# State-space norm: squares of the prompt columns summed between the two halves of the heads' products, sample columns handled apart

## What is computed

```python
# Mamba-2
y = y + xs * D_skip
y = y.reshape(B, T, SSM_DIM) * silu(z)
yg = y.reshape(B, T, SSM_GROUPS, SSM_DIM // SSM_GROUPS)            # 2 groups of 512 channels
yg = yg * rsqrt(mean(yg * yg, axis=-1, keepdims=True) + NORM_EPS)
out = yg.reshape(B, T, SSM_DIM) * norm_w
# RWKV-7, per head of 64 channels
yn = (y - mean(y)) * rsqrt(var(y) + RW_LN_EPS) * ln_w + ln_b
out = (yn + bonus) * g
```

## Time and profile before

| | |
|---|---|
| median of 3 runs | 4482.1 us (4466.71 to 4493.42) |
| profiled execution | 4487.48 us, its span 4485.9 us |
| busy over the span | PE 94%, PEld 85%, DVE 72%, ACT 32%, POOL 35% |
| mean granted clock of TensorE over the span | 0.969 |
| changed function | 1253.2 to 1394.0 us |
| busy in 1253.2 to 1394.3 | PE 96.7, PEld 59.0, DVE 69.4, ACT 67.8, POOL 37.5 us |
| granted clock of TensorE in it | 0.69 |

### The profile page before, as it was taken

One profiled execution on the slowest core, in us unless ns is written; L12 is line 12 of the kernel. 1 busy time (PEld: TensorE's weight loads), 2 busy tenths in 40 slices (PEclk: granted clock), 3 DMA queues, 4 the chain that ended last, 5 costly groups with the idle time before them and its releaser, 6 DMA issues. The chain is left out here.

```text
span 4485.9 us, 85731 instructions
## 1 busy us (share of the span) xinstructions
PE 4205.8 (94%) x32575; PEld 3817.0 (85%) x32575; DVE 3225.6 (72%) x6008; ACT 1431.1 (32%) x2183; POOL 1565.5 (35%) x1316
## 2 busy tenths in 40 slices
PE   7989998999768979999999998899999999999997
PEld 4888887888546868978878887899999999999996
DVE  5631344555844237899985664999999999999997
ACT  2211222111634222233346765222222222222223
POOL 6333333564031200044443323444343443433431
PEclk9999999999868989999999999999999999999998
DMA  4655665455543311134434455999999999999994
GB/s 169 201 193 187 203 226 205 172 200 182 138 140 97 130 73 39 39 127 143 143 125 174 174 210 190 331 302 299 301 300 302 301 302 295 304 303 296 305 299 158
DMA packets 523006, 928.01 MB, mean 207 GB/s; under 512 B 284032, under 2 KB 351232, under 8 KB 518688
## 3 DMA queue, kind: packets, MB, share of 16 engines
q1 hardware_dynamic: 387024, 549.29, 37.3%
q0 software_dynamic: 80960, 346.96, 22.6%
q10 hardware_dynamic: 54816, 28.85, 2.2%
HBM read 785.79 MB, written 206.30 MB: 221 GB/s over the span
## 5 line engine op out<-in xcount | busy, mean ns | idle before, releaser
L3271 POOL DMA_INDIRECT ex_rows<-expert_rows,ex_here x512 | 588.0, 1148 | 952.2 <-DVE acc_tok L3406 861.0
L3406 DVE SCALAR_TENSOR_TENSOR acc_tok<-ex_rows,ex_wsp,acc_tok 128x1024 f32<-128x1024 f32 x512 | 633.5, 1278 | 0.0
L2650 PE MATMUL ex_psa<-x_dense_high,eg_u_high 128*128 128x288 f32 x2048 | 604.5, 295 | 13.9 <-DVEq L3460 13.9
L2741 POOL TENSOR_TENSOR eg_u_low<-eg_u,eg_u_high 128x1024 fp32r<-128x1024 f32 x130 | 330.0, 2539 | 808.4 <-ACT eg_u_high L2736 808.4
L2650 PE MATMUL ex_psa<-x_dense_low,eg_u_high 128*128 128x288 f32 x2048 | 604.5, 295 | 0.0
L2650 PE MATMUL ex_psa<-x_dense_high,eg_u_low 128*128 128x288 f32 x2048 | 604.2, 295 | 0.0
L3303 PE MATMUL ex_pso<-ex_w_high,ex_v_high 128*128 128x288 f32 x2048 | 441.4, 297 | 11.7 <-DVE acc L3388 6.6
L3334 ACT ACTIVATE ex_w<-ex_psa 128x288 f32<-128x288 f32 x256 | 105.5, 412 | 1062.8 <-PE ex_psa L2650 1060.3
L3303 PE MATMUL ex_pso<-ex_w_high,ex_v_low 128*128 128x288 f32 x2048 | 440.0, 297 | 0.0
L3303 PE MATMUL ex_pso<-ex_w_low,ex_v_high 128*128 128x288 f32 x2048 | 438.9, 296 | 0.0
L3388 DVE TENSOR_TENSOR acc<-ex_pso,acc 128x576 f32<-128x576 f32 x512 | 373.7, 750 | 47.9 <-PE ex_pso L3303 47.9
(11 more groups left out here) (514 smaller groups left out, 9533.7 us busy)
## 6 DMA issues: line engine op xcount, KB each, us to landing
eg_u<-in_u SPq DMA_DIRECT2D x256, 512.0 KB, 3.3
expert_rows<-in_v SPq DMA_DIRECT2D x128, 512.0 KB, 7.0
ex_v<-in_v SPq DMA_DIRECT2D x128, 512.0 KB
weights<-wt_stage SPq DMA_DIRECT2D x9, 4096.0 KB, 12.2
ex_g<-weights SPq DMA_DIRECT2D x128, 288.0 KB
expert_rows<-eg_act SPq DMA_DIRECT2D x256, 128.0 KB, 1.7
proj<-in_out POOLq DMA_DIRECT2D x50, 548.5 KB, 6.2
in_w<-in_w_in SPq DMA_DIRECT2D x50, 512.0 KB, 4.7
```

Source lines behind the costliest of these rows:

```text
L2650: yield nc.tensor.matmul(out[:, 0:b - a], w[:, kc, :], half[:, kc, a:b], start=n == 0, stop=n == len(passes) - 1)
L2741: self.k.nc.gpsimd.tensor_tensor(self.ul[par][:, :, :], self.u[par % 2][:, :, :], self.uh[par][:, :, :].bitcast(F32), ALU.subtract).then_i ...
L3271: pool.indirect_dma_start(rows[i][:, :], None, table, index(here[par][:, t, j:j + 1]), element_offset=ROW_RUNS[t][0]).then_inc(s_row[i], 16)
L3406: v.scalar_tensor_tensor(out=acc_tok[:, t, :], in0=rows[i][:, at:at + D], scalar=wsp[:, i:i + 1], in1=acc_tok[:, t, :], op0=ALU.mult, op1= ...
```

## The change

The prompt columns and the sample columns of the Mamba-2 norm are parted. The squares of the prompt columns go in place over silu(z), which is no longer needed once a tile is gated (so no buffer is waited for), and their sums into two PSUM banks of 512 columns. The samples' squares are made in one instruction, summed in eight products of 64 columns into the bank that held the heads' result, and scaled in eight small instructions of their own. The arena is only as large as the sample recurrence needs. The orders are rewritten: on SP the load of S comes first; on TensorE the heads run in two halves of eight with only `mean(0)` between them, then `var(0)` and the first four sums with `mean(1)`, then the states; on ScalarE the centred square of pair 0 and two squares stand behind sigmoids 0 to 3, sigmoids 4 to 7 come before `rw_rstd(0)`; on VectorE "skip" comes before `gated(0)`.

```diff
@@ -1807,10 +1807,12 @@
         col = sb("col", [P, 3, SH])
         cb = sb("cb", [P, SG, L])
         btok = sb("btok", [P, SG, SN])
-        arena = sb("arena", [P, 3 * T])
+        arena = sb("arena", [P, SH * (SD + 2 * L)])
         heads_of = lambda at, n: arena[:, at:at + SH * n].rearrange("p (h m) -> p h m", h=SH)
         xt, w, ce = heads_of(0, SD), heads_of(SH * SD, L), heads_of(SH * (SD + L), L)
-        sq, rs = [arena[:, i * T:(i + 1) * T] for i in range(2)], arena[:, 2 * T:3 * T]
+        sq = [z[:, i, 0:SEQ] for i in range(KC)]
+        rs = [z[:, GT * g, 0:SEQ] for g in range(SG)]
+        sq_s, rs_s = z[:, :, SEQ:T], z[:, 0:SG, SEQ:T]
         xd = sb("xd", [P, SH, SD])
         end = sb("end", [P, NSEQ, SH])
         xm = [sb(f"xm{i}", [P, SH, SD]) for i in range(2)]
@@ -1818,11 +1820,12 @@
         rw_rs = sb("rw_rs", [P, T])
         ps = ctx.enter_context(nc.psum_tensor("ss_ps", [P, 2, 512], F32))
         ps_so3 = ctx.enter_context(nc.psum_tensor("po_so_ps", [P, 3, 512], F32))
-        ps_so, ps_rw = banked(ps_so3), banked(ctx.enter_context(nc.psum_tensor("po_rw_ps", [P, 3, 512], F32)))
+        ps_so, ps_rw = flat(ps_so3[:, 1:3, :]), banked(ctx.enter_context(nc.psum_tensor("po_rw_ps", [P, 3, 512], F32)))
         cview = ps[:, 0, 0:3 * SH].rearrange("p (q h) -> p q h", q=3)
         bcv = ps[:, 1, :].rearrange("p (i g m) -> p i g m", i=2, g=SG)
         xv = ps_so3[:, 0:2, :].rearrange("p a b -> p (a b)").rearrange("p (h m) -> p h m", h=SH)
         yv = ps_so3[:, 0, :].rearrange("p (a l) -> p a l", a=KC)
+        sum_s = ps_so3[:, 0, 0:SG * L]
         s_S = k.sem("ss_state_loaded")
         s_out = k.sem("ss_state_stored")
         s_xm = k.sem("ss_masked_x")
@@ -1832,7 +1835,9 @@
         s_skip = k.sem("ss_y_gated")
         s_gp = k.sem("so_prompt_gated")
         s_r = k.sem("so_rstd_step")
-        s_n = k.sem("so_scaled")
+        s_sq = k.sem("so_samples_squared")
+        s_sum = k.sem("so_samples_summed")
+        s_rs = k.sem("so_samples_rstd_step")
         PE = Progress(k.sem("ss_pe"), "col", "bc", "x", "y")
         AC = Progress(k.sem("ss_act"), "excs", "col", "btok", "dec")
         DV = Progress(k.sem("ss_dve"), "cb", "x", "diff", "end", "ce", "xd", "w", "skip")
@@ -1848,8 +1853,8 @@
         with nc.Block() as block:
             @block.sync
             def _(sp):
+                sp.dma_start(S[:, :, :, :].rearrange("p s h m -> p s (h m)"), io["ssmT"].rearrange("s n m -> n s m")).then_inc(s_S, 16)
                 rw_post_load(k, sp, 0, y, gate, bonus)
-                sp.dma_start(S[:, :, :, :].rearrange("p s h m -> p s (h m)"), io["ssmT"].rearrange("s n m -> n s m")).then_inc(s_S, 16)
                 rw_post_load(k, sp, 1, y, gate, bonus)
                 mw.load(sp, 0, mw.wa, mw.wb, mw.s_w)
                 for p_ in range(2, NPAIR):
@@ -1896,7 +1901,16 @@
                     pe.wait_ge(SQ.sem, SQ.done("sq", i))
                     if i == GT:
                         pe.wait_ge(s_r, 1)
-                    product(ps_so, k.ones[:, :], sq[i % 2], i % GT == 0, i % GT == GT - 1).then_inc(*SP.inc("sum"))
+                    for a, b in ((0, 512), (512, SEQ)):
+                        mm = nc.tensor.matmul(ps_so[:, a:b], k.ones[:, :], sq[i][:, a:b], start=i % GT == 0, stop=i % GT == GT - 1)
+                    mm.then_inc(*SP.inc("sum"))
+
+                def total_samples():
+                    pe.wait_ge(s_sq, 1)
+                    for i in range(KC):
+                        mm = nc.tensor.matmul(sum_s[:, L * (i // GT):L * (i // GT) + L], k.ones[:, :], sq_s[:, i, :],
+                                              start=i % GT == 0, stop=i % GT == GT - 1)
+                    mm.then_inc(s_sum, 1)
 
                 def heads(lo, hi):
                     for i in range(lo, hi):
@@ -1928,38 +1942,37 @@
                 for i in range(KC):
                     mm = nc.tensor.transpose(xv[0:L, 2 * i:2 * i + 2, :].rearrange("p h m -> p (h m)"), inx[:, i, :], k.ident[:, :])
                 mm.then_inc(*PE.inc("x"))
-                mean(0)
                 pe.wait_ge(s_S, 16)
                 at(DV, "w")
-                heads(0, 4)
+                heads(0, 8)
+                mean(0)
+                heads(8, 16).then_inc(*PE.inc("y"))
                 var(0)
-                heads(4, 8)
+                total(0)
+                total(1)
                 mean(1)
-                heads(8, 12)
-                var(1)
-                heads(12, 16).then_inc(*PE.inc("y"))
-                mean(2)
+                total(2)
+                total(3)
                 at(AC, "btok")
                 at(DV, "xd")
                 states(0)
-                total(0)
                 states(1)
-                total(1)
+                var(1)
+                total(4)
+                total(5)
+                total_samples()
+                mean(2)
+                states(2)
+                states(3)
+                total(6)
+                total(7)
                 var(2)
-                states(2)
-                total(2)
-                states(3)
+                states(4)
+                states(5)
                 mean(3)
-                total(3)
-                states(4)
-                total(4)
-                states(5)
+                states(6)
+                states(7)
                 var(3)
-                total(5)
-                states(6)
-                total(6)
-                states(7)
-                total(7)
 
             @block.scalar
             def _(act):
@@ -1991,17 +2004,24 @@
 
                 def square(i):
                     act.wait_ge(s_gp, i + 1)
-                    if i >= 2:
-                        act.wait_ge(SP.sem, SP.done("sum", i - 2))
-                    a.activation(sq[i % 2], ob[:, i, :], ACT.Square).then_inc(*SQ.inc("sq"))
+                    a.activation(sq[i], ob[:, i, 0:SEQ], ACT.Square).then_inc(*SQ.inc("sq"))
+
+                def square_samples():
+                    act.wait_ge(s_skip, 1)
+                    a.activation(sq_s, ob[:, :, SEQ:T], ACT.Square).then_inc(s_sq, 1)
 
                 def so_rstd(g):
                     act.wait_ge(SP.sem, SP.done("sum", GT * g + GT - 1))
-                    if g:
-                        act.wait_ge(s_n, GT)
-                    a.activation(rs, ps_so[:, 0:T], ACT.Ln, scale=1.0 / (GT * P), bias=k.const[:, 0:1]).then_inc(s_r, 1)
+                    a.activation(rs[g], ps_so[:, 0:SEQ], ACT.Ln, scale=1.0 / (GT * P), bias=k.const[:, 0:1]).then_inc(s_r, 1)
                     act.wait_ge(s_r, 2 * g + 1)
-                    a.activation(rs, rs, ACT.Exp, scale=-0.5).then_inc(s_r, 1)
+                    a.activation(rs[g], rs[g], ACT.Exp, scale=-0.5).then_inc(s_r, 1)
+
+                def so_rstd_samples():
+                    act.wait_ge(s_sum, 1)
+                    a.activation(rs_s, sum_s.rearrange("p (g l) -> p g l", g=SG), ACT.Ln, scale=1.0 / (GT * P),
+                                 bias=k.const[:, 0:1]).then_inc(s_rs, 1)
+                    act.wait_ge(s_rs, 1)
+                    a.activation(rs_s, rs_s, ACT.Exp, scale=-0.5).then_inc(s_rs, 1)
 
                 act.wait_ge(smp.s_in, 48)
                 a.activation(ce, csb[:, :, :], ACT.Exp).then_inc(*AC.inc("excs"))
@@ -2014,40 +2034,41 @@
                 sigmoid(1)
                 at(DV, "diff")
                 a.activation(w[0:L, :, :], w[0:L, :, :], ACT.Exp).then_inc(*AC.inc("dec"))
-                centered_square(0)
                 sigmoid(2)
                 sigmoid(3)
-                rw_rstd(0)
-                centered_square(1)
+                centered_square(0)
+                square(0)
+                square(1)
                 sigmoid(4)
                 sigmoid(5)
-                rw_rstd(1)
+                square(2)
+                square(3)
+                sigmoid(6)
+                sigmoid(7)
+                rw_rstd(0)
+                square_samples()
                 at(DV, "xd")
                 masked_x(0)
                 masked_x(1)
-                sigmoid(6)
-                sigmoid(7)
-                centered_square(2)
-                act.wait_ge(s_skip, 1)
-                square(0)
-                square(1)
-                masked_x(2)
-                rw_rstd(2)
-                masked_x(3)
-                square(2)
-                square(3)
-                masked_x(4)
-                centered_square(3)
-                masked_x(5)
+                centered_square(1)
                 so_rstd(0)
                 square(4)
                 square(5)
-                rw_rstd(3)
-                masked_x(6)
-                masked_x(7)
+                rw_rstd(1)
+                masked_x(2)
+                masked_x(3)
+                centered_square(2)
                 square(6)
                 square(7)
                 so_rstd(1)
+                so_rstd_samples()
+                rw_rstd(2)
+                masked_x(4)
+                masked_x(5)
```

(45 more changed lines are left out.)

## The result

| | before | after |
|---|---|---|
| median of 16 runs | 4492.36 us (4466.71 to 4499.72) | 4505.24 us (4487.78 to 4512.72) |
| ratio after / before | | 1.0029, 95% interval 1.0019 to 1.0039 |
| profiled execution, its span | 4487.48, 4485.9 us | 4506.03, 4504.4 us |
| changed function | 1253.23 to 1394.27: 141.0 us | 1252.30 to 1413.89: 161.6 us |
| granted clock in it | 0.69 | 0.62 |

The kernel became 12.9 us slower, 0.29%. Most of the difference between the forecast of 4494 and the measured 4505.24 is the base: the three runs that the forecast started from had a median of 4482.1, the sixteen have 4492.36. The difference itself was forecast at +11.4 and measured at +12.9. In the two profiled executions the function differs by more, 20.6 us, 9 us above the forecast. Where those 9 us come from is the subject of much of what follows; why the medians show less of them stays open in part.

What follows compares the result with a forecast made beforehand. No engine bounds the function; a chain of releases hopping between engine queues does. Its six legs from 1269.6 end the block at 1405.4, 11.4 us later than before, giving 4494 us (+0.27%), range 4468 to 4512.

Steps and rivals of the forecast that it cites:

- Start: SP's load of S, now issued first, lands near 1266; heads then wait for VectorE's `w` and start 2.1 us earlier.
- Leg 1: Heads to `center(0)`: eight uninterrupted heads at the low clock, 2.21 us each, then `mean(0)` and `center(0)`; 22.9 us.
- Rival 2: Clock rises in unbroken heads: six of the first eight take 1.28 us, `mean(0)` 2.0; total 4486; chance 0.06.
- Leg 2: ScalarE from the centred square through squares, table loads and four sigmoids to `rw_rstd(0)`; 21.6 us.
- Leg 3: VectorE from `gated(0)` to `center(1)`: 7.6 us of work plus 8.0 of exclusion by POOL's decays of S; 15.6 us.
- Leg 4: ScalarE from `center(1)` to `gated(1)`: squares, `so_rstd(0)` and `rw_rstd(1)`, with TensorE and VectorE work hidden; 12.7 us.
- Legs 5 and 6: `gated(1)` through `rw_rstd(2)`, 27.3 us; then `gated(2)` to the block's end, 35.7 us, TensorE's clock partly low.
- rival 3: TensorE's broken tail stays at the low clock, `states(3)` held up by 6 us; +25, total 4507; chance 0.17.
- Rival 4: New order does what it is arranged for, waits overlap; block ends 7.6 us earlier, total 4475; chance 0.10.

Runs made afterwards that it cites:

- one-element decays: Changed kernel with POOL's eight decays of S cut to one element each (sample states then wrong); 4491.61 us, ratio 1.0001 to the kernel before.
- additions first: Changed kernel with add_state(4) ahead of gated(2) and scale(1), and the samples' rstd and scaling later; 4493.26 us, ratio 1.0013 to before.
- tail filled: Changed kernel with 13 unread products of 512 columns put into TensorE's idle time in the tail; 4495.99 us, ratio 1.0015 to before.
- decays later: Changed kernel with POOL's decays held until gate_prompt(5) is done; 4503.16 us, ratio 1.0050 to the kernel before.
- rearranged kernels: Two kernels keeping the changed kernel's split, with norm products between heads and additions ahead of scalings; 4463.15 and 4455.89 us, ratios 0.9941 and 0.9939 to before.
- rearranged further: First of the rearranged kernels with gated(1) ahead of the skip and total(2) ahead of the last four heads; 4455.89 us, ratio 0.9939 to before.

## Why the prediction held, step by step

The legs of the prediction beside the same stretches in the profile of after, each from the end of one named instruction to that of the next; all from the start of the heads, forecast at 1269.6 and found at 1268.8 in a function that began 0.9 us earlier.

| leg | forecast | measured |
|---|---|---|
| 1: eight heads, `mean(0)`, `center(0)` | 22.9 | 22.9 |
| 2: ScalarE, to the rstd of pair 0 | 21.6 | 23.9 |
| 3: VectorE beside the decays | 15.6 | 15.7 |
| 4: to the rstd of pair 1 | 12.7 | 12.7 |
| 5: to the rstd of pair 2 | 27.3 | 29.0 |
| 6: to the end | 35.7 | 40.6 |
| sum | 135.8 | 144.8 |

**Start.** As said: the load of S goes out first, at 1252.3, and lands in time, after 12.8 us, and VectorE's `w` is what releases the heads.

**Leg 1.** As said, to 0.1 us: 2.2 us a head, and `mean(0)` at the low level. Rival 2, a clock that rises inside unbroken heads, falls: the windows have 0.50 over 39.2 us in which TensorE never idles. The rule cited from the Trainium skill, "TensorE: Matmul & The Clock Gate", Part 1, disagrees with the trace here: the heads do not lift the clock.

**Leg 2.** Two errors of opposite sign. No table was loaded between the squares and `sigmoid(4)`: 1.3 us less. But the last eight heads were all slow, where the sum had three fast ones, and `var(0)` was slow too; the Ln waited 3.66 us for it. In the profiles of four variants with the same two halves of heads (one-element decays, additions first, tail filled, decays later) three of those heads were mostly at the high level; in none of the three profiles of the changed kernel itself. Nothing in these kernels ahead of the heads differs, so this too is left open.

**Leg 3.** As said: 8 us of exclusion, in five instructions. The trace of before had only plain products against POOL; the normalising form behaves the same. The parts of the 8 us were off and made up for each other: the forecast had 0.4 us for the first instruction and 1.9 for each of four, and all five waited 1.5 to 1.7. The statement of the Trainium skill, "GPSIMD Engine Reference", Specifications, that two SBUF inputs are enough for contention, agrees with the trace: 2.87 to 3.00 us instead of 1.2 to 1.35 for each of them. The run with one-element decays showed the 8 us to lie on the path.

**Leg 4.** As said.

**Legs 5 and 6.** The releases came as said: `states(1)`, `(3)` and `(5)` each wait for VectorE, for 9.48, 3.89 and 6.32 us. The step that was mis-sized is the clock. `total(6)` and `total(7)` took 5.69 us and not 3.7, `states(5)` and `mean(3)` together 7.0 and not 5.7, the last three pieces 11.1 and not 7.5. Together 6.9 us, less 0.3 in smaller terms: rival 3 by half. The last three pieces even cost more than the forecast's own price for the low clock, which was 9.8 and should have been 11.1: that is what they took at the low level throughout. Its first part (a slow `total(4)` and `total(5)`, then 6 us of delay for `states(3)`) did not come: the two took 3.60 us. The tail filled with products showed the clock to be a cost by itself.

**The sum.** 9.0 us more than forecast in this profile, nearly all of it TensorE at the lower level. In the medians only 1.5 more, 12.9 against 11.4. The chain was worked out for the function and missed its length by 9 us; that the medians hid most of the miss is luck, and why they did is not known.

**Rival 4** fell with this order. What the change set out to use is there all the same: the rearranged kernels keep its buffers and its parted columns, and gain 0.6%. How much of that the free buffers are worth was not tried apart from the orders.

## What to carry to other kernels

In a stretch that no engine bounds, walk the written orders as one chain of releases, queue by queue, and ask of every instruction placed ahead of a wait who stands behind it: a state addition queued behind 10 us of gating and scaling cost more (8.5 us in the profile) than half of an 18 us stall whose successor was held up anyway (1 us). Put VectorE's instructions with two SBUF inputs where POOL is idle, under other work if there is any, and not at the point where a long POOL queue has just been released. And profile the unchanged kernel more than once where TensorE's clock changes within the stretch: here its length moved by 8 us between two profiles, as much as the exclusion cost.

## What the runs showed of the hardware

- VectorE and POOL took turns, one whole instruction each, as long as both had instructions with two SBUF inputs: 1.35 becomes 2.87 to 3.00, 1.2 becomes 2.9, four scalings go from 4.87 to 10.09. POOL's eight decays took 15.4 us where hardly anything met them (rearranged further), 16.3 before, and 18.5 to 20.5 elsewhere. VectorE instructions with a PSUM input kept their 1.28 us (`center(2)` at 1325.95 before).
- The heads ran at a granted clock of 0.50 through 39 us in which TensorE had no gap. Behind `mean(0)` three heads ran mostly at the high level in four kernels and none in three executions of the changed one; with sums and means between every four heads, the last eight did in one kernel (2.2 us became 1.3) and six of them in another.
- ScalarE loaded no table between Square and Sigmoid, but did between every Ln and the Exp behind it, 1.28 us each time.
- The same kernel's function of 141 us took 149.4 in one of three profiles, mostly through TensorE's clock from `total(0)` on; the rest of the program varied by up to 26 us between profiles, whichever kernel ran.
